# Where the tokens of an expert stand among 64 rows: two runs from the two ends in place of steps of four

## The reference, cut to what matters

```python
lg = (t @ p['w_router_group'] + p['b_router_group']).astype(F32)
grp = jnp.argmax(lg, axis=-1)
le_g = jnp.take_along_axis(le, grp[:, None, None], axis=1)[:, 0]
pe = jax.nn.softmax(le_g, axis=-1)
top_p, top_i = lax.top_k(pe, TOP_K)
wts = p_grp * top_p / jnp.sum(top_p, axis=-1, keepdims=True)
ids = grp[:, None] * EXPERTS_PER_GROUP + top_i
...
for e in range(N_EXPERTS):
    z = jax.nn.silu(t @ p['w1'][e]) * (t @ p['w3'][e])
    y = y + gates[:, e:e + 1] * (z @ p['w2'][e])
```

```
group 0: 11 17  7 16 50 14 27 38
group 1:  9 20 15 14 14  8 11 17
group 2: 46 33 47 32 28 24 37 49
group 3: 20 41 24 34 14 22 11 18
```

## Time and profile before

| | us |
|---|---|
| median of three runs | 1010.91 |
| lowest and highest | 1010.44, 1012.23 |
| the profiled execution, its own time | 1011.33 |
| its span in the profile | 1009.6 |

### The profile page before, as it was taken

How to read it: one execution, slowest core, us unless ns; L and a number is a source line. 1 busy time by engine, 2 the same in 40 slices (tenths; PEclk the granted TensorE clock), 3 DMA queues, 4 the chain that set the end, 5 groups by cost and what they waited for, 6 DMA issues and landing times.

```text
span 1009.6 us, 10937 instructions
## 1 busy us (share of the span) xinstructions
PE 838.3 (83%) x4234; PEld 523.7 (52%) x4234; DVE 346.1 (34%) x535; ACT 263.0 (26%) x439; POOL 250.5 (25%) x207
## 2 busy tenths in 40 slices
PE   3898898998999999996988887778778867886850
PEld 1688786987999999545333332232323222332320
DVE  2599695859103442266111111111111111111106
ACT  4384535572334332112111111111111111111113
POOL 0047261635355554000111110111111011101000
PEclk9799998999999999996999999998999988999995
DMA  9994172646563447726599999999999999999714
GB/s 345 360 320 139 32 253 97 237 167 222 182 211 137 170 171 235 302 108 246 193 401 407 414 415 415 418 421 400 405 405 417 393 421 400 413 412 412 330 80 187
DMA packets 69171, 295.10 MB, mean 292 GB/s; under 512 B 8549, under 2 KB 19077, under 8 KB 56837
## 3 DMA queue, kind: packets, MB, share of 16 engines
q1 hardware_dynamic: 62740, 284.40, 72.7%
q0 software_dynamic: 5120, 6.31, 1.9%
q10 hardware_dynamic: 1264, 3.76, 1.0%
HBM read 290.20 MB, written 14.72 MB: 302 GB/s over the span
## 4 chain that ended last, share of the span: by engine, by line
PE 51%; DMA 27%; DVE 15%; ACT 4%; issue 2%; SPq 1%; DVEq 0%; POOLq 0%; POOL 0%; ACTq 0%
DMA ring<-in_w 14%; DMA slot<-in_w 10%; PE bank L937 7%; PE bank L793 7%; PE bank L795 7%; PE bank L794 7%; PE bank L924 6%; PE bank L923 6%; PE bank L845 3%; DVE xcy L1469 3%; DMA ring<-in_w_ada 2%; DVE lru L1777 2%; PE bank L741 1%; ACT lru L1313 1%; DVE lru L1523 1%
## 5 line engine op out<-in xcount | busy, mean ns | idle before, releaser
L457 POOL TENSOR_TENSOR subs<-ring,subs 128x1024 fp32r<-128x1024 f32 x69 | 176.7, 2568 | 221.1 <-ACT subs L1044 221.1
L793 PE MATMUL bank<-h_hl,subs 128*128 128x384 f32 x488 | 168.0, 344 | 12.0 <-ACT lru L1123 4.5
L795 PE MATMUL bank<-h_hl,subs 128*128 128x384 f32 x488 | 166.0, 340 | 0.0
L794 PE MATMUL bank<-h_hl,subs 128*128 128x384 f32 x488 | 165.9, 340 | 0.0
L923 PE MATMUL bank<-ring,x_T 128*64 128x512 f32 x256 | 116.6, 610 | 22.7 <-DMA ring<-in_w 11.4
L1777 DVE TENSOR_TENSOR lru<-bank,lru 64x512 f32<-64x512 f32 x32 | 32.8, 1025 | 272.2 <-ACT lru L1313 272.2
L924 PE MATMUL bank<-ring,x_T 128*64 128x512 f32 x256 | 118.7, 618 | 0.0
L640 POOL COPY idx<-lists 64x1 uint32 (+1 forms) x32 | 5.7, 178 | 410.0 <-PE bank L909 331.9
L793 PEld LDWEIGHTS bank<-h_hl,subs 128*128 128x128 f32 x488 | 93.0, 190 | 19.2 <-issue 9.5
L923 PE MATMUL bank<-slot,x_T 128*64 128x512 f32 x192 | 88.2, 614 | 16.6 <-DMA slot<-in_w 10.9
L1044 ACT ACTIVATE subs<-ring 128x1024 fp32r<-128x1024 f32 x72 | 76.1, 1059 | 67.1 <-PE bank L795 66.1
(11 more groups left out here) (222 smaller groups left out, 1237.4 us busy)
## 6 DMA issues: line engine op xcount, KB each, us to landing
ring<-in_w SPq DMA_DIRECT2D x48, 2048.0 KB, 31.3
slot<-in_w SPq DMA_DIRECT2D x36, 2048.0 KB, 31.2
ring<-in_w_in SPq DMA_DIRECT2D x14, 2048.0 KB, 8.2
ring<-in_w_ada SPq DMA_DIRECT2D x12, 2048.0 KB, 9.2
gate_w<-in_w SPq DMA_DIRECT2D x12, 2048.0 KB, 31.9
ring<-in_w_rnn_out SPq DMA_DIRECT2D x2, 2048.0 KB, 8.5
ring<-in_w_conv_out SPq DMA_DIRECT2D x2, 2048.0 KB, 8.0
ring<-in_w_o SPq DMA_DIRECT2D x2, 2048.0 KB, 8.3
```

What stands on the lines that cost most here:

```text
L457: eng.tensor_tensor(pair[:, 1], src, pair[:, 0].bitcast(F32), ALU.subtract).then_inc(done, 1)
L793: eng.matmul(ps[:, 0:T], pair[:, 1, k, :], x[:, 0, k, :], start=(k == 0), stop=False)
L794: eng.matmul(ps[:, 0:T], pair[:, 0, k, :], x[:, 1, k, :], start=False, stop=False)
L795: mm = eng.matmul(ps[:, 0:T], pair[:, 0, k, :], x[:, 0, k, :], start=False, stop=(k == KD - 1))
```

## The change

The table with which the rank is compared is now made for each token beforehand, at the end of `choose(t)`. For a token whose expert is one of the first four of its group, it is the plain count 0 to 63, and the token of rank r lands in row r. For one of the last four it is 63 minus the count, and the token lands in row 63 - r. The table is written into `rank_oh` itself, and `place(t)` compares it in place. Nothing else is altered: the lists, the loop, the DMAs and their number are the same.

```diff
@@ choose(t), behind tok_oh
+                eng.tensor_scalar(r[:, 50:52], r[:, 44:46], float(EG // 2), float(CAP - 1), ALU.is_ge, ALU.mult)
+                then(eng.tensor_scalar(r[:, 52:54], r[:, 44:46], float(EG // 2), 2.0, ALU.is_lt, ALU.mult))
+                then(eng.tensor_scalar(r[:, 52:54], r[:, 52:54], -1.0, None, ALU.add))
+                for k in range(2):
+                    last = eng.tensor_scalar(rank_oh[:, t, k, :], iota[:, 0:CAP], r[:, 52 + k:53 + k],
+                                             r[:, 50 + k:51 + k], ALU.mult, ALU.add)
+                then(last)
@@ place(t)
                 for k in range(2):
-                    last = eng.tensor_scalar(rank_oh[:, t, k, :].rearrange("p (b a) -> p b a", a=CAP // 16),
-                                             iota[:, 0:CAP].rearrange("p (a b) -> p b a", b=16),
-                                             rank[:, t, k:k + 1], None, ALU.is_equal)
+                    last = eng.tensor_scalar(rank_oh[:, t, k, :], rank_oh[:, t, k, :], rank[:, t, k:k + 1],
+                                             None, ALU.is_equal)
```

## The result

| | before | after |
|---|---|---|
| median, us | 1010.67 (four runs, 1009.99 to 1012.23) | 1002.91 (four runs, 1002.49 to 1003.87) |
| span of the profiled execution, us | 1009.6 | 1002.0 |

The ratio is 0.9922 (95% interval 0.9905 to 0.9940): 7.8 us or 0.78% faster. The forecast was 1012.1 with a range of 1008.6 to 1014.9.

A forecast was written before the change was run, and what follows sets the result against it. The expert loop was taken to go at the pace of the DMA queues. Routing 0.9, queues 0.0 and last scatter 0.3 summed to +1.2 us on 1010.9, so 1012.1 us, with a range of 1008.6 to 1014.9.

The forecast's parts named there:

- part 3: DMA queues in the expert loop: five more copies on the fullest engine, +0.85, against -0.9 given back; sum 0.0 us.
- A: Experiments' theory: row bits 1 to 4 name the DMA engine, and the fullest of sixteen sets the pace; 180 copies before.
- The price of a copy: Expert loop: one 4096-byte row copy costs 0.17 us from below, 0.35 us from above by the pace of light and heavy experts.
- the bound of -1.8 us: Expert loop: most given back if the slope's second half follows the fuller engines' mean load, 10.5 copies at 0.17 us.
- The third: Rival, DMA rows: engine n has rows n, n + 16, n + 32, n + 48; -24 us, so 988; chance 0.04.
- The second rival: DMA queues: gathers by engines n and n + 8 add up through shared doors; -1.5 to -3.1 us; chance 0.18.
- The first rival: Engine 0's queue: the fullest engine alone sets the pace, nothing given back; +3.2 us, so 1014.1; chance 0.24.
- Part 1: Routing: five added VectorE instructions cost 0.95 us a tile, of which 0.9 us in all is exposed.
- move as one: Behind the routing, the lists, four unused matmuls and transposes shift together; nothing added for the clock, half a microsecond either way.
- Part 2: First gather, expert 0: 0.5 us more for three rows on one engine is hidden; gathers in the loop aren't late.
- Part 4: Last scatter, 18 tokens: at most 2 rows on an engine before, 4 after; +0.3 us.
- theory E: Experiments' theory, DMA queues: copies of one DMA crowding on few engines cost all engines more.

The follow-up runs named there:

- engines mirrored for half of the experts: Steps of two by table, only row bits 1 to 4 mirrored for half of the experts, seven routing instructions added, against the kernel before: 1000.03 us, ratio 0.9903.
- steps of two: Kernel before with a constant table putting ranks in rows 0, 2, 4 ... 62, then 1, 3 ..., no added routing work: 998.04 us, ratio 0.9885; repeated 997.60.
- pairs: Kernel before with a constant table: neighbouring ranks in two neighbouring rows, these twos four rows apart, no added work: 1011.33 us, ratio 1.0010.
- the run with rows 0, 32, 2, 34: Kernel before with a constant table putting ranks 0, 1, 2, 3 ... in rows 0, 32, 2, 34 ..., no added work: 1005.03 us, ratio 0.9951.
- the run with the work alone: Changed kernel with its five added routing instructions, but comparing against the old table, so tokens stand in steps of four: 1010.80 us, ratio 1.0005 to before.
- steps of four with two ends: Changed kernel with the old steps of four in its table, from row 0 for half of the experts, from row 63 for the others: 1000.47 us, ratio 0.9897.
- steps of sixteen: Kernel before with a constant table putting ranks 0 to 3 in rows 0, 16, 32, 48, then 1, 17 ..., no added work: 1022.28 us, ratio 1.0123.

## Why the prediction was wrong

**The step that failed** is in part 3: "I take it that they are four neighbouring rows, engine n having rows 4n to 4n + 3". The count of 80 packets gave only that an engine has four rows; which four was assumed, and the sum of part 3, 0.0 within -1.8 to +1.75, hung on it. Under it the old steps had 123 copies on the fullest engine and the new runs 128, and the change could give little. Under A they were bad, 180 copies where a level load has 93, and the change takes 82 copies off the fullest engine. At the price of 0.17 us that the prediction took for a copy from the page, this would be 14 us; 8.35 were measured. The table says why it isn't more: from 180 to 121 copies the time from restart to take-up falls by 11.6 us, and below 121 it falls no further, so near the level load the fullest engine no longer sets the time alone. It isn't the count by itself: with the scatters left out, where a level load is 48, going from 94 to 63 copies still gave 6.6 us. One candidate that the traces show is TensorE. With engines mirrored for half of the experts its chain runs over TensorE from 924.98 us on, in part at half clock, and expert 31's second matrix had landed 0.8 us before it was taken up at 956.21. No run isolates this.

**The price of a copy** was bounded rightly: 0.17 from below, 0.35 from above, 0.19 measured. The upper bound came from the wrong engine's count: the light stretch has 13 copies on A's fullest engine, not 8, and the heavy one 69, not 47, which makes the slope 0.72 / (6.9 - 4.3) = 0.28. The doubling that I read as "something that the copies of other engines cause" was thus the wrong count in some part, 0.07 of the 0.18 us above the lower bound, and the bound of -1.8 us, of which the sum took half, had no row of its own.

**The rivals.** The third, rows dealt out otherwise, was the right kind of case, and had 0.04. It tried one other deal, rows 16 apart, and refused the whole kind with it. That refusal stood on a wrong count too: counted between the same ends as the 8 and 47 copies, the light stretch has 21 copies under that deal and not 25, 7.0 an expert against 7.7 in the heavy one, so the pace should have risen a little and not fallen. The deal is refused by the runs: under it steps of two and pairs both have 180 copies, and they lie 13 us apart. The completion times of the sixteen parts in the trace before could have refused neighbouring rows, as they show two groups of eight with 16 us between them, while under neighbouring rows the counts fall from 123 to 65 without a gap. The second rival, shared doors, was to give 1.5 to 3.1 us. Rows 32 apart do meet, but on one engine and not, as it had it, through two engines n and n + 8. The Trainium skill's page "DMA: Bandwidth & Descriptors", section "The descriptor swizzle", gives for a transfer of 128 partitions that one engine has rows 0 to 3 and 32 to 35; that rows 32 apart share an engine agrees with the run with rows 0, 32, 2, 34 (0.9951, as with neighbouring rows). The page doesn't tell the deal of 64 rows. The first rival, the fullest engine alone, was right as a mechanism down to 121 copies of this kernel and had the sign of the change in load wrong.

**Part 1** was right in its first half. Its 0.95 us a tile measured 1.05; from the start of the last norm's L1666 to L890 it is 15.49 us (476.36 - 460.87); the run with the work alone has 15.62 (475.98 - 460.36). Before it was 476.21 after a norm at 461.63, 14.58, so 0.9 and 1.0 later, as summed. Behind it "move as one" isn't so. The unused matmuls took 4.85 and 4.76 us in place of 5.27; the granted clock from 480 to 490 us is 0.87 and 0.90 in place of 0.83, so it rose at an earlier one of them. The added work needn't be the reason: in the runs without it the same matmuls took 4.65 to 5.42 us, with it 4.35 to 5.46. From norm to restart it is 30.73 (491.60 - 460.87) against 30.25: 0.5 us, as the device time of the run with the work alone shows (+0.5, between -0.6 and +1.5).

**Part 2** held: gathers landed in 2.7 to 10.4 us and nothing waited for them.

**Part 4** was wrong in sign: the scatter took 2.58 us in place of 3.39. Under A the 18 tokens in steps of four put three rows on each of two engines and two on six, and in the new runs no engine has more than two. But that isn't the reason, or not alone: pairs put four rows on one engine and steps of four with two ends again three, and their scatters took 2.49 and 2.46 us. The old placement with the work added repeated 3.40, steps of sixteen took 3.19, and the cause stays open.

**Not foreseen** was the 1.7 us at the end, where the last w2 matmuls ran in part at half the clock. It isn't the change's alone: the run with steps of two has a granted clock of 0.66 from 960 to 965 us, in the same matmuls.

## What to carry to other kernels

Where a DMA moves few rows beside a full queue, ask for the load of each engine and not for the sum: first find out from a trace or from a few placements which rows belong to one engine, and only then count. The cheapest remedy here wasn't the change but another constant table: steps of two from row 0 need no added work and gave 998.0 and 997.6 us, 5 us less than the changed kernel and 12 less than the one before. Once the fullest engine was down to 121 copies, with a level load at 93, more levelling bought nothing.

## What the runs showed of the hardware

An indirect DMA over 64 partitions was dealt out so that rows 2j, 2j + 1, 2j + 32 and 2j + 33 belong to one DMA engine (j from 0 to 15): of the fifteen ways to name the engine by four of the row's six bits, this one fits the order of the placements that start at row 0, but for pairs and steps of four, which measure alike. A row of 4096 bytes on the fullest engine cost 0.19 us under a full queue, from 121 to 244 copies; gathers and scatters both count, and whether equally isn't shown. Engines ran up to 23 us apart on one queue, no further even with 0 and 244 copies, and the program waited for the last of them.

Where the full engines lie matters too: with their order reversed, and with it that of the moved rows, the time rose by 3.5 us. This would explain why kernels that mirror half of their experts gain nothing beyond steps of two, but that is argued and not shown; whether some engines have less room, and from what, wasn't tried and stays open. Open is also why the change's runs of neighbours (-7.8) stay behind the other placements with two ends (-10.4 and -11.1), within intervals of about 2 to 3 us each and with loops of 465.56, 465.20 and 464.00 us; theory E would give such an order, and no run isolates it.
